# A hybrid encoder step: the order of a table stage, y's place in a scan, its clears, and an inversion split five to three

## The reference, cut to what matters

```
sa = S @ a_t
S  = S * w_t + outer(sa, b_t) + outer(v_t, k_t)
y_t = S @ r_t
```

## Time and profile before

| | us |
|---|---|
| median of 3 runs (3702.57 to 3711.77) | 3711.1 |
| the profiled execution, its own time | 3706.92 |
| its span | 3705.1 |

### The profile page before, as it was taken

One profiled execution on the slowest core, in us unless ns is written; L12 is line 12 of the kernel. 1 busy time (PEld: TensorE's weight loads), 2 busy tenths in 40 slices (PEclk: granted clock), 3 DMA queues, 4 the chain that ended last, 5 costly groups with the idle time before them and its releaser, 6 DMA issues. The chain is left out here.

```text
span 3705.1 us, 60364 instructions
## 1 busy us (share of the span) xinstructions
PE 3483.0 (94%) x25902; PEld 3269.3 (88%) x25902; DVE 1544.6 (42%) x2525; ACT 1130.6 (31%) x2105; POOL 604.5 (16%) x713
## 2 busy tenths in 40 slices
PE   8899979999999999998899876987999999999998
PEld 8898769989999999994698776865998999999997
DVE  6335464343332332335236657656334332232233
ACT  6223263223221221225435522544223321121123
POOL 1100112002110110121211365422100210010012
PEclk9999989999999999998899987998999999999999
DMA  6412311202111111115646666963200111111111
GB/s 227 109 59 66 106 30 53 71 18 47 46 46 46 46 46 46 46 35 170 214 144 215 201 176 161 254 143 88 91 29 24 46 46 46 46 46 49 46 43 66
DMA packets 457386, 323.09 MB, mean 87 GB/s; under 512 B 105134, under 2 KB 435215, under 8 KB 453871
## 3 DMA queue, kind: packets, MB, share of 16 engines
q1 hardware_dynamic: 402874, 280.72, 26.3%
q10 hardware_dynamic: 43876, 18.99, 2.0%
q0 software_dynamic: 10368, 19.51, 1.6%
HBM read 232.29 MB, written 86.96 MB: 86 GB/s over the span
## 5 line engine op out<-in xcount | busy, mean ns | idle before, releaser
L83 PE MATMUL ps<-am_y,am_wh 128*128 128x352 f32 x4944 | 1182.3, 322 | 12.4 <-PEq L2579 12.4
L83 PE MATMUL ps<-am_h,am_wh 128*128 128x352 f32 x3648 | 884.1, 324 | 1.1 <-DVE am_h L1412 1.1
L83 PEld LDWEIGHTS ps<-am_y,am_wh 128*128 128x128 f32 x4944 | 855.8, 188 | 14.7 <-issue 13.4
L83 PE MATMUL ps<-am_y,am_wl 128*128 128x352 f32 x2472 | 792.4, 321 | 0.0
L83 PEld LDWEIGHTS ps<-am_h,am_wh 128*128 128x128 f32 x3648 | 636.7, 188 | 4.2 <-DVE am_h L1412 1.4
L83 PE MATMUL ps<-am_h,am_wl 128*128 128x352 f32 x1824 | 588.6, 323 | 0.0
L83 PEld LDWEIGHTS ps<-am_y,am_wl 128*128 128x128 f32 x2472 | 463.9, 188 | 0.0
L83 PEld LDWEIGHTS ps<-am_h,am_wl 128*128 128x128 f32 x1824 | 342.7, 188 | 0.0
L1500 POOL TENSOR_TENSOR am_silu<-am_silu,rs 128x352 f32<-128x352 f32 x132 | 126.7, 962 | 1229.3 <-ACT am_silu L1356 1229.3
L1082 DVE TENSOR_TENSOR x<-ps,x 128x352 f32<-128x352 f32 x240 | 125.9, 524 | 462.4 <-PE ps L83 456.9
L83 PE MATMUL ps<-rw_parts,rw_wh 128*128 128x352 f32 (+1 forms) x1152 | 289.5, 333 | 24.5 <-PEq L2561 13.1
(11 more groups left out here) (327 smaller groups left out, 4614.7 us busy)
## 6 DMA issues: line engine op xcount, KB each, us to landing
am_w<-in_ffn_w SPq DMA_DIRECT2D x120, 512.0 KB, 3.9
rw_ra_d<-tb_rk SPq DMA_DIRECT2D x8, 1056.0 KB, 8.2
rw_kbt_d<-tb_gk SPq DMA_DIRECT2D x8, 1056.0 KB, 4.0
rw_gg_d<-tb_gk SPq DMA_DIRECT2D x8, 1056.0 KB, 6.2
fr_w<-in_xa_wk SPq DMA_DIRECT2D x8, 1024.0 KB, 5.4
fr_w<-in_xa_wv SPq DMA_DIRECT2D x8, 1024.0 KB, 5.3
am_w<-in_xa_wq SPq DMA_DIRECT2D x16, 512.0 KB, 3.9
am_w<-in_xa_wo SPq DMA_DIRECT2D x16, 512.0 KB, 3.9
```

The costliest lines, as they stand in the source:

```text
L83: mm = nc.tensor.matmul(out, l, part, start=start and n == 0, stop=stop and n == 2)
```

## The change

Six edits, all in `tables` and `delta_scan`.

1. The table stage's order. ScalarE's `tile_highs(2)` moves from the end of step 7 to step 8, behind `put(0)`; VectorE's eight low halves of that block move from the end of step 7 to step 8, behind `put_g(p, 1)`.
2. VectorE's substitution steps are spread anew; none stand in step 8 or among the copies of step 9.
3. SP's `load_triangles(1)` moves from ahead of `store_v(0)` to behind it.
4. The batches are pairs 0 to 4 (110 partitions, three matrices each) and 5 to 7 (102 partitions, two each, the 33 chunks padded to 34 by a copy of chunk 0, two small DMAs more for each of three pairs). In batch 1 both engines take both matrices of a partition, but VectorE rows 4 and up (steps i = 4 to 30) and GpSimd rows 0 to 3 (31 steps). ScalarE's queue stores batch 0 with 10 DMAs, batch 1 goes out with 3 and 3.
5. In the scan, two of y's eight pairs stay ahead of u, six go between u and the state's addition; the wait for tt stands ahead of y.
6. Each slot of tt and v is cleared whole, by two memsets: slot 0 on VectorE ahead of the state's memset, slots 1 and 2 on GpSimd ahead of their tt loads. GpSimd's tt loads wait for the clear of tt, SP's v loads of the first three loads for that of v; PE no longer waits for clears.

```diff
+        def clear(ops, at):
+            ops.memset(tt[:, at], 0.0).then_inc(tt_cleared[at], 1)
+            ops.memset(v[:, at], 0.0).then_inc(v_cleared[at], 1)
...
+                if l < SLOTS:
+                    sp.wait_ge(v_cleared[l], 1)
                 for h in range(2):
                     sp.dma_start(v[h * HD:h * HD + C, l % SLOTS, :, 0:w, :],
...
                 if l >= SLOTS:
                     pool.wait_ge(y_done, last(l - SLOTS) + 1)
+                elif l:
+                    clear(nc.gpsimd, l)
+                if l < SLOTS:
+                    pool.wait_ge(tt_cleared[l], 1)
...
-                if l < 2:
-                    pe.wait_ge(cleared, (7, 14)[l])
...
-                y_part(n, lambda p: S[:, p, :], lambda p: ra[:, s, p, 1], True)
                 pe.wait_ge(tt_in[l % SLOTS], tt_due(l))
                 for q in range(2):
+                    if q == 0:
+                        y_part(n, lambda p: S[:, p, :], lambda p: ra[:, s, p, 1], True, range(2))
                     pe.wait_ge(z_out, 2 * n + q + 1)
...
                     mm.then_inc(u_done, 1)
+                y_part(n, lambda p: S[:, p, :], lambda p: ra[:, s, p, 1], True, range(2, PAIRS))
...
-QUADS = 2
+BATCHES = ((0, 5, 3), (5, 8, 2))
+PADDED = NCH + 1
...
+    per, share, top = [n for _, _, n in BATCHES], 2, 4
+    lanes = [2 * (hi - lo) * (NCH + NCH % n) // n for lo, hi, n in BATCHES]
...
+            lo, hi = ((0, share), (share, per[0]))[n] if q == 0 else (0, per[1])
+            r0, r1 = (0, i + 1) if q == 0 else ((top, i + 1), (0, min(i + 1, top)))[n]
...
                 if u >= 0:
                     if u == 1:
-                        load_triangles(sp, 1)
-                    if u == 1:
                         sp.wait_ge(b_done, PAIRS)
                     if u + 1 < PAIRS and u >= 1:
                         sp.wait_ge(bonus_done, u)
                         load_beta(sp, u + 1)
                     if u >= 1:
                         store_v(sp, u - 1)
+                    if u == 1:
+                        load_triangles(sp, 1)
             store_v(sp, PAIRS - 1)
-            store_triangles(sp, 1, range(4))
+            store_triangles(sp, 1, range(3))
...
                 put(0)
+                if u == 0:
+                    tile_highs(2)
...
-                if s == V0 - 1:
-                    tile_highs(2)
                 if u == 6:
-                    store_triangles(act, 0, range(8))
+                    store_triangles(act, 0, range(10))
...
-                if u == 1:
-                    steps(2, 5)
                 if prepares(s):
                     floor(q)
                 if crosses(s):
                     put_g(p, 1)
-                if u == 1:
-                    steps(5, 7)
+                if u == 0:
+                    for k in range(KT):
+                        tile_low(dve, nc.vector, (2 * BLOCKS - 1) * KT + k)
...
                 if u >= 0:
-                    steps(*((0, 2), (8, 12), (12, 19), (19, 27), (27, 35), (35, 43), (43, 50), (50, 57))[u])
+                    steps(*((0, 0), (0, 3), (3, 11), (11, 18), (18, 27), (27, 37), (37, 45), (45, 52))[u])
             bonus(PAIRS - 1)
-            steps(57, 2 * (C - 1))
+            steps(52, 2 * (C - 1) - top)
```

More of the change, by code:

```diff
@@ L527, in z_part, with y_part @@
                 return mm
-            def y_part(n, lhs, rhs, start):
-                for p in range(PAIRS):
+            def y_part(n, lhs, rhs, start, pairs=range(PAIRS)):
+                for p in pairs:
                     at = p // 2 * HD
@@ L584, in _ @@
         def _(dve):
+            clear(nc.vector, 0)
             nc.vector.memset(state[:, 0], 0.0).then_inc(init_set, 1)
[L586 to L594, removed]
             dve.wait_ge(init_turned, 1)
@@ L1919, in set_eyes @@
             pool.wait_ge(blanked, q + 1)
-            for n in range(per):
-                nc.gpsimd.memset(eyes[q][:, n * C:n * C + (C - 1) * (per * C + 1) + 1:per * C + 1], 1.0).then_inc(eyes_set[q], 1)
+            for n in range(per[q]):
+                nc.gpsimd.memset(eyes[q][:, n * C:n * C + (C - 1) * (per[q] * C + 1) + 1:per[q] * C + 1], 1.0).then_inc(eyes_set[q], 1)
         def store_triangles(eng, q, xs):
             for n in range(2):
-                eng.wait_ge(added[n], (C - 1) * (q + 1))
+                eng.wait_ge(added[n], steps_done(n, q, C - 1))
@@ L1927, in store_triangles @@
+            lo, hi, _ = BATCHES[q]
+            rows = lanes[q] // (2 * (hi - lo))
             for x_ in xs:
[L1928 to L1934, removed]
-                eng.wait_ge(inv_in[q], 16)
[L1936 to L1942, removed]
+                h, p = x_ // (hi - lo), lo + x_ % (hi - lo)
+                eng.dma_start(tt_d[p % 2, h, :, p // 2, 0:rows * per[q]].rearrange("s (g a) t -> g s (a t)", a=per[q]),
+                              rows_x[q][x_ * rows:(x_ + 1) * rows]).then_inc(inv_out, 16)
@@ new lines, in substitute @@
+        def substitute(eng, ops, n, q, i):
+            lo, hi = ((0, share), (share, per[0]))[n] if q == 0 else (0, per[1])
+            r0, r1 = (0, i + 1) if q == 0 else ((top, i + 1), (0, min(i + 1, top)))[n]
+            t_ = top_t if q and n else inv_t[:, lo:hi]
+            if i == (top if q and not n else 0):
+                eng.wait_ge(inv_in[q], 16)
+                eng.wait_ge(eyes_set[q], per[q])
+            r, w, m, before = r1 - r0, C - 1 - i, hi - lo, steps_done(n, q, i)
+            t = t_[0:lanes[q], :, 0:r * w].rearrange("l a (r w) -> l a r w", r=r)
+            if before:
+                eng.wait_ge(added[n], before)
+            ops.tensor_tensor(t, inv_x[q][:, lo:hi, r0:r1, i:i + 1].broadcast_to([lanes[q], m, r, w]),
+                              inv_m[q][:, lo:hi, i:i + 1, i + 1:C].broadcast_to([lanes[q], m, r, w]), ALU.mult)\
@@ L1943, in substitute @@
                 .then_inc(outer[n], 1)
[L1944 to L1945 removed]
+            eng.wait_ge(outer[n], before + 1)
+            block_ = inv_x[q][:, lo:hi, r0:r1, i + 1:C]
             ops.tensor_tensor(block_, block_, t, ALU.add).then_inc(added[n], 1)
```

50 lines of the change are left out of this document (26 added, 24 removed).

## The result

The changed kernel is slower. Its median is 3721.39 us (3716.88 to 3727.82, 7 runs) against 3710.36 (3702.57 to 3711.77, 7 runs) for the kernel before; the ratio is 1.0038, 95% interval 1.0029 to 1.0047. The slowdown is small, but clear of the noise. The profiled execution has a span of 3722.3 us (3705.1 before).

The account below looks back on a forecast made before the run. PE, 94% of the span, was taken as the bound. Savings of 28.5 us in tables, 1.9 at the scan's start and 3.3 from y sum to 33.7: 3673 from 3706.92, put at 3676, range 3660 to 3696.

Parts of the forecast that it names:

- Term 1: PE's first wait in tables, 13.29 us: moving `tile_highs(2)` brings the sums forward to about 2107.5, 9.1 us saved.
- the clock's price: PE's sums after its first wait, 3.88 us at the low clock against 2.04 steady: up to 1.8 more, none counted.
- Terms 2 and 3: PE's second and third waits in tables, 7.36 and 11.38 us: 9.0 us saved on the second, 10.4 on the third.
- Term 4: End of tables: the inversion keeps up with PE, last step about 2248.5, so tables ends 28.5 us earlier, at 2263.
- Term 5: Scan's start: PE's 1.85 us wait for the start state's copy goes, as VectorE has fewer clears; 1.9 us saved.
- Term 6: y's place in the scan: six moved pairs fill PE's hole, 0.1 us gained per chunk, 3.3 over 33 chunks.
- A: Rival in the scan: y's new place costs up to 0.15 us a chunk, +5, total about 3683; chance 0.15.
- B: Rival in tables: VectorE's and GpSimd's operations lie end to end, inversion still ends tables; 3690 to 3701, chance 0.12.
- C: Rival in the scan: new holes keep PE at the low clock, 2.0 us more per chunk, up to 3735; chance 0.04.
- D: Rival in tables: nothing moves, PE stands for each pair's vt stores instead; 3700 to 3710, chance 0.06.

Follow-up runs that it names:

- the one cut: The changed kernel with each of the last batch's six stores cut into two, 16 partitions and 1: 3681.74 us, ratio 0.9925 to the kernel before.

## Why the prediction was wrong

The forecast was 3676, with a chance of 0.88 for faster. The kernel as changed came out at 3721.4, above the range and at the upper end of what the prediction called the same (3700 to 3722, 0.08). With the one cut it is 3681.7. There the scan starts 27.8 us earlier than before, of 28.5 booked, and what is left to the forecast is about the 5.2 us of terms 5 and 6.

- **Term 1** held. A wait of about 4 was said, 3.97 measured, and undoing the move costs 12.4 against the 9.1 booked. The sums took 3.50 in place of 3.88, so next to nothing of the clock's price was saved, as assumed.
- **Terms 2 and 3** held as waits: gone, and 0.54 where 0 to 4 was said. Undone together they bring 8.62 and 11.79 back. That costs 13.6 by the medians, less than the 19.4 booked, but 23.3 at the scan's first issue in the profiled execution, more than that. So their size is known only to within some 10 us.
- **Term 4 failed, and by one clause**: "the final stores are three per queue instead of four: -1.5". Measured, they cost 25.85 more issue time on SP alone (31.75 against 5.90), and 51.2 us instead of 12.0 from the inversion's end to the scan's first issue: +39.2. I priced a store by its count and its size, and never asked into how many parts its outer dimension divides. The rest of the term was near: VectorE's last step ended at 2254.95, for 2248.5 with 2255 as the limit. The stores of batch 0 did delay `put_vt(6)`, and PE stood 4.19 us for it; sharing them changed nothing, so that sits beside the path.
- **Term 5**: the wait of 1.85 is gone, and worth 0 of the 1.9 booked. **Term 6**: 0.07 to 0.08 a chunk instead of 0.10, and 0 of the 3.3. Both edits made PE's own chain shorter, and the stage's length didn't follow. My bounds asked only what PE and VectorE do, and I read PE's busy 137 of 147 us as proof that nothing else counts; the 3.6 us for which PE stood for its instructions were in that trace already.
- **The rivals**: A and B didn't come: the period fell, and the inversion ended by the 2255 that was said, not at 2280.5. (One sign of B, the inversion's addition as the last work in tables, did come, as it stood before.) C, the low clock for the whole scan, didn't either: 0.98 was granted from 2334 to 2480. D is excluded by the waits. No rival had the stores: the one that ended slower looked at PE's clock, not at the piece of the change that makes new transfers with a new shape.
- **The Trainium skill's rule on the shared port** (SBUF — State Buffer, "SBUF: two separate sides"), which I weighed against term 4: by it the split by rows buys no overlap. The new batches are worth 13.2, and VectorE's operations in the second one take 27.1 us in place of 43.0, so the rule did not decide. Batch 0 speaks neither for it nor against it. Its operations have the same shapes per partition before and after, yet VectorE's 62 took 41.7 us before and 47.5 after, while GpSimd was at work for 0.89 and 0.90 of that time. With the change's order and 88 partitions they took 46.4, so it isn't the number of partitions; the cause is not shown.

## What to carry to other kernels

For each new DMA, look at the size of its outer dimension on both sides before its bytes: 17 partitions went through a path of 18 GB/s, 11 through one of 140, and cutting 17 into 16 and 1 was worth 40 us. In a profile the sign is an idle stretch with a DMA share near 0.08 and few GB/s, with issues on SP and ScalarE that take some seven times as long as like ones (10.6 us each against 1.5). A gain booked on one engine's wait only counts if the stage's other chain comes earlier too, so undo parts singly and compare their sum with the whole. And where PE waits without a releaser, look at the packets of the "instruction" queue.

## What the runs showed of the hardware

- Stores with 17 partitions, in 256-byte runs, went out at 17 to 18 GB/s together, whether three came from one queue or six from two. From the inversion's end to the scan it took 51.2, 30.0 and 13.3 us with six, three and none of them.
- With 9 and 8 partitions the tail is as short as with 16 and 1 (12.8 and 13.3 us). The issues take 6 to 8 us a queue in both; that they set the tail fits, but no run shows it.
- An idle engine doesn't mean an idle issuer: SP and ScalarE needed 31.75 and 28.14 us to issue three stores each.
- PE can stand for its own instructions in a stage that is dense with transfers: 40 waits of up to 2.07 us in five scans, each ending 1.2 to 1.6 us after a 16 KB packet of the "instruction" queue has landed. In the chunk behind one of 1.96 us the granted clock was 0.71.
